# A two-block transformer layer on one core: pass loop folded into one, low weight parts multiplied first, the router's chain rearranged behind the last output fill, and each quad's first up half placed in front of its predecessor's spreading

## The reference

```python
h = h + merged @ w_out[l]
h = h + hier_moe(rms_norm(h, norm2_g[l]), w_router_group[l], b_router_group[l],
                 w_router_expert[l], b_router_expert[l], w_expert_in[l], w_expert_out[l])
return rms_norm(h, norm_f_g)

def hier_moe(...):                        # 4 groups of 8 experts, 2 experts per token
    g_sel = argmax(xt @ w_group + b_group)
    top_v, top_i = top_k(e_logits of the chosen group, 2)
    gates = g_prob * softmax(top_v)
    hdn = ragged_dot(xs, w_e_in, group_sizes)      # 32 experts, 1024 -> 2 x 256
    act = silu(gate_h) * up_h
    ys = ragged_dot(act, w_e_out, group_sizes)     # 256 -> 1024, times the gate, added to the token
```

## Time and profile before

| what | value |
|---|---|
| runs of the kernel | 960.22, 959.97, 955.93 us; median 959.97 |
| profiled execution | 960.35 us, of which the trace's span is 958.6 us |
| busy: PE, DVE, ACT, POOL | 858.6, 497.6, 391.0, 92.2 us |
| DMA | 217.57 MB, mean 227 GB/s |
| TensorE's granted clock, mean | 0.958 of full |

### The profile page before, as it was taken

How to read it: one execution, slowest core, us unless ns; L and a number is a source line. 1 busy time by engine, 2 the same in 40 slices (tenths; PEclk the granted TensorE clock), 3 DMA queues, 4 the chain that set the end, 5 groups by cost and what they waited for, 6 DMA issues and landing times.

```text
span 958.6 us, 14713 instructions
## 1 busy us (share of the span) xinstructions
PE 858.6 (90%) x5971; PEld 708.3 (74%) x5971; DVE 497.6 (52%) x779; ACT 391.0 (41%) x534; POOL 92.2 (10%) x111
## 2 busy tenths in 40 slices
PE   4889999899999986786668799999989899999996
PEld 3889789799997532332232698998888699999995
DVE  5798577654564311101010566455557557666674
ACT  5323453456342311101112455454643456566362
POOL 1032000111000000000001401111152000000000
PEclk9899999899999998987889799999999999999999
DMA  7755454224688999999999964424434816655611
GB/s 216 257 164 208 176 176 176 89 93 171 229 326 324 414 421 421 421 422 423 422 420 377 225 137 147 176 89 175 89 138 142 269 65 200 220 173 175 219 44 44
DMA packets 94392, 217.57 MB, mean 227 GB/s; under 512 B 14663, under 2 KB 45509, under 8 KB 82049
## 3 DMA queue, kind: packets, MB, share of 16 engines
q1 hardware_dynamic: 93649, 215.32, 61.9%
q10 hardware_dynamic: 576, 1.18, 0.4%
q0 software_dynamic: 112, 0.30, 0.3%
HBM read 215.44 MB, written 1.34 MB: 226 GB/s over the span
## 4 chain that ended last, share of the span: by engine, by line
PE 62%; DMA 16%; DVE 11%; ACT 4%; issue 4%; SPq 3%; POOL 0%; DVEq 0%; ACTq 0%
PE ps L826 14%; PE ps L828 14%; PE ps L827 14%; DMA moe_ring<-in_w_expert_in 14%; PE ps L1230 6%; PE ps L1147 5%; DVE w_lo L1607 3%; DMA stage<-in_w_in 1%; PE ps L985 1%; DMA stage_b<-in_w_up 1%; SPq L694 1%; ACT w_hi L1311 1%; PE ps L1179 1%; PE ps L1169 1%; PE ps L970 1%
## 5 line engine op out<-in xcount | busy, mean ns | idle before, releaser
L828 PE MATMUL ps<-x_hi,w_lo 128*128 128x256 f32 x664 | 189.8, 286 | 0.0
L828 PEld LDWEIGHTS ps<-x_hi,w_lo 128*128 128x128 f32 x664 | 129.5, 195 | 0.0
L1607 DVE TENSOR_TENSOR w_lo<-stage,w_hi 128x2048 fp32r<-128x2048 f32 (+1 forms) x44 | 101.8, 2354 | 32.1 <-ACT w_hi L1311 30.9
L826 PE MATMUL ps<-x_hi,w_hi 128*128 128x256 f32 x360 | 105.6, 293 | 8.8 <-DVE w_lo L1607 8.2
L1311 ACT ACTIVATE w_hi<-stage 128x2048 fp32r<-128x2048 f32 (+1 forms) x44 | 79.1, 1848 | 61.0 <-PE ps L828 51.7
L827 PE MATMUL ps<-x_lo,w_hi 128*128 128x256 f32 x360 | 103.9, 289 | 0.0
L826 PE MATMUL ps<-x_hi,w_odd 128*128 128x256 f32 x312 | 89.1, 285 | 1.3 <-DVE x_lo L1598 1.3
L828 PE MATMUL ps<-x_hi,w_odd 128*128 128x256 f32 x312 | 88.3, 283 | 0.0
L827 PE MATMUL ps<-x_lo,w_odd 128*128 128x256 f32 x312 | 88.3, 283 | 0.0
L826 PE MATMUL ps<-x_hi,w_lo 128*128 128x256 f32 x304 | 86.6, 285 | 0.0
L827 PE MATMUL ps<-x_lo,w_lo 128*128 128x256 f32 x304 | 86.0, 283 | 0.0
(11 more groups left out here) (381 smaller groups left out, 1915.6 us busy)
## 6 DMA issues: line engine op xcount, KB each, us to landing
stage<-in_w_in SPq DMA_DIRECT2D x23, 2048.0 KB, 8.1
moe_ring<-in_w_expert_in SPq DMA_DIRECT2D x44, 1024.0 KB, 18.1
moe_ring<-in_w_expert_out SPq DMA_DIRECT2D x20, 1024.0 KB, 19.4
stage_b<-in_w_up SPq DMA_DIRECT2D x12, 1024.0 KB, 8.6
stage<-in_w_down SPq DMA_DIRECT2D x11, 1024.0 KB, 5.0
stage<-in_w_up SPq DMA_DIRECT2D x10, 1024.0 KB, 9.5
up_odd<-in_w_expert_in SPq DMA_DIRECT2D x8, 1024.0 KB, 22.1
down_odd_a<-in_w_expert_out SPq DMA_DIRECT2D x6, 1024.0 KB, 21.0
```

Source lines behind the costliest of these rows:

```text
L826: mm(out, still[0], moving[0], start=first, stop=False)
L828: return mm(out, still[1], moving[0], start=False, stop=last)
L1607: tt(lo[:, cols], staged(n)[:, cols], hi[:, cols].bitcast(fp32), ALU.subtract).then_inc(lo_ready, 1)
```

## The change

1. SP's loads: `up_odd_c` lies at 160 KiB (before at 96), and is loaded with `up_odd_d` once `merged_ready` is 4; `wide_g` takes its place at 100 KiB, over tile 1 of h_tok, and is loaded by ACT behind the residuals. The second pair of quad 0's down pieces and one half of down_odd_b wait for a new semaphore `wo_read`.
2. The fourth wo fill multiplies in another order: the 8 products with w_lo first, then those with x_lo, then the high ones; after the first and the second eight, wo_read is raised. The same 9 products as before stand between the router's steps.
3. `route()`: PE takes the first half of the logits of tile 1 before the transposes; the rank's products are handed over one by one; three of the four residuals stand behind the first up half of quad 0. ACT takes tile 0's xs_tok before it squares tile 1; POOL adds EPS ahead.
4. The first up half of quad q+1 (`first_half`) stands in front of the spreading of quad q.
5. PE's passes are one loop whose count is 1 at first and is read from npass_i before the last two quads; an `If(r > 0)` holds the gather and first half that later passes need. The other engines keep the second copy.

```diff
-    steps.append({"op": "wopart", "k": range(0, 2)})
+    steps.append({"op": "wopart", "k": range(0, 6)})
     at("xt", 2)
-    steps.append({"op": "wopart", "k": range(2, 3)})
+    steps.append({"op": "wopart", "k": range(6, 9)})
...
             eng.wait_ge(merged_ready, 4)
-            load_up(1, 1, 0, range(3, 4))
+            load_up(1, 1, 0, high)
             wait_split(eng, units_one - 1)
             load_up(0, 0, 0, high)
             eng.wait_ge(pj_full, units[units_one - 2]["read"])
             load_up(0, 0, 1, low)
             load_down(0, 0, low)
+            eng.wait_ge(wo_read, 1)
+            load_down(0, 0, high)
+            eng.wait_ge(wo_read, 2)
+            load_down(1, 1, range(3, 4))
             eng.wait_ge(pj_full, units[units_one - 1]["read"])
             load_up(0, 0, 1, high)
-            load_down(0, 0, high)
-            load_down(1, 1, high)
-            eng.wait_ge(routed_xs, 2)
-            eng.wait_ge(residual_in, 4)
-            load_up(1, 1, 0, range(2, 3))
+            load_down(1, 1, range(2, 3))
             load_rest(0)
...
+            def wo_last(products):
                 n = where["wo", 3]
+                w = parts(split_pair(units_one - 1))
...
+                for at in products:
+                    k = at % KT
+                    b, f = ((0, 1), (1, 0), (0, 0))[at // KT]
+                    last = mm(ps[:, n % 4, :], (x_hi, x_lo)[b][:, k, P:2 * P], w[f][:, k, 0:BANK],
+                              start=(at == 0), stop=(at == 3 * KT - 1))
+                    if k == KT - 1 and at // KT < 2:
+                        last.then_inc(wo_read, 1)
...
                 eng.wait_ge(sel_ready, 1)
+                mm(ps[:, 1, 0:32], tri[:, 0:P], chosen[:, 0, :], start=True, stop=True).then_inc(rank_full, 1)
+                wait_read(eng, "at", "xt", 1)
+                router_logits(3, 1, range(0, 4))
                 eng.wait_ge(h_ready, 4)
-                mm(ps[:, 2, 0:32], tri[:, 0:P], chosen[:, 0, :], start=True, stop=True).then_inc(rank_full, 1)
...
+                for half in range(2):
+                    eng.wait_ge(xt_copied, half + 1)
+                    last = router_logits(3, 1, range(4 + 2 * half, 6 + 2 * half))
+                last.then_inc(lg_full, 1)
...
+            def first_half(it, p):
+                eng.wait_ge(act_ready, it + 1)
+                eng.wait_ge(xg_a, it + 1)
+                eng.wait_ge(moe_in[(0, 4)[p]], it * 32 + (64, 32)[p])
+                up_half(p, 0).then_inc(up_a, 1)
...
+                if not final:
+                    first_half(it + 1, 1 - p)
                 eng.wait_ge(spread_ready, it + 1)
...
-                def quads(r):
+                def quads(r, count):
                     with eng.Fori(0, QUADS // 2 - 1) as i:
                         for p in range(2):
                             quad(r, i * 2 + p, p)
+                    eng.wait_ge(npass_ready, 1)
+                    eng.reg_load(count, npass_i[0:1, 0:1])
                     quad(r, QUADS - 2, 0)
                     quad(r, QUADS - 1, 1, True)
-                quads(0)
-                eng.wait_ge(npass_ready, 1)
-                passes = eng.value_load(npass_i[0:1, 0:1], min_val=1, max_val=S // CAP)
-                with eng.If(passes > 1):
-                    with eng.Fori(1, passes) as r:
+                first_half(0, 0)
+                for b in range(1, 4):
+                    residual(b // 2, b % 2)
+                count = eng.alloc_register("passes")
+                eng.reg_mov(count, 1)
+                with eng.Fori(0, count) as r:
+                    with eng.If(r > 0):
                         gather(r * QUADS, r * QUADS + 1)
-                        quads(r)
+                        first_half(r * QUADS, 0)
+                    quads(r, count)
...
+                    if t == 0:
+                        eng.wait_ge(half_squares, NT)
+                        step(eng.tensor_scalar(half_ms, ss_half[:, 0:2 * NT:2], EPS, None, ALU.add))
                     eng.wait_ge(half_squares, 3 + t)
-                    step(eng.tensor_tensor(ms[:, one], ss_half[:, 2 * t:2 * t + 1], ss_half[:, 2 * t + 1:2 * t + 2], ALU.add))
-                    step(eng.tensor_scalar(ms[:, one], ms[:, one], EPS, None, ALU.add))
+                    step(eng.tensor_tensor(ms[:, one], ss_half[:, 2 * t + 1:2 * t + 2], half_ms[:, one], ALU.add))
```

More of the change, by code:

```diff
@@ L1063, in route @@
                 eng.wait_ge(sel_ready, 2)
-                mm(ps[:, 2, 32:64], tri[:, P:S], chosen[:, 0, :], start=True, stop=False)
-                mm(ps[:, 2, 32:64], tri[:, 0:P], chosen[:, 1, :], start=False, stop=True)
-                mm(ps[:, 2, 64:96], tri[:, P:S], chosen[:, 0, :], start=True, stop=False)
-                mm(ps[:, 2, 64:96], tri[:, P:S], chosen[:, 1, :], start=False, stop=True).then_inc(rank_full, 1)
-                residual(1, 0)
+                mm(ps[:, 2, 0:32], tri[:, 0:P], chosen[:, 1, :], start=False, stop=True).then_inc(rank_full, 1)
+                for t in range(NT):
+                    last = mm(ps[:, 3, 0:32], tri[:, P:S], chosen[:, t, :], start=(t == 0), stop=(t == 1))
+                last.then_inc(rank_full, 1)
+                residual(0, 0)
                 eng.wait_ge(pick_ready, 1)
@@ L1121, in gather, with up_half @@
                     last.then_inc((gather_a, gather_b)[half], 1)
+            def up_half(p, half, final=False):
+                for kk in range(4):
+                    k = 4 * half + kk
+                    for j in range(QUAD):
+                        last = mm(ps[CAP * j:CAP * (j + 1), 2, :], xg[p][:, k, CAP * j:CAP * (j + 1)],
+                                  expert_up(p, half, j, final)[:, kk, :], start=(k == 0), stop=(k == KT - 1),
+                                  skip_group_check=True)
+                return last
@@ new lines, in quad @@
+                if not final:
+                    gather(it + 1, it + 1)
+                eng.wait_ge(gate_pick_ready, it + 1)
+                eng.wait_ge(actf_ready, it + 1)
+                for t in range(NT):
+                    last = eng.transpose(ps[:, 3, t * P:(t + 1) * P],
+                                         pick_gate[:, t, :, :].rearrange("p e c -> p (e c)"), ident[:, :])
+                last.then_inc(spread_full, 1)
+                eng.wait_ge(xg_b, it + 1)
+                if final:
+                    eng.wait_ge(up_last_in, r * 64 + 64)
+                else:
+                    eng.wait_ge(moe_in[1], r * (64 * (QUADS - 1)) + q * 64 + 64)
@@ L1821, in route @@
                 eng.wait_ge(rank_full, 1)
-                step(stt(rank[:, 0, :], chosen[:, 0, :], far, ps[:, 2, 0:32], ALU.mult, ALU.add))
+                step(stt(rank[:, 0, :], chosen[:, 0, :], far, ps[:, 1, 0:32], ALU.mult, ALU.add))
                 pick_slots(0, 0).then_inc(first_picked, 1)
-                eng.wait_ge(xt_full, 1)
-                eng.tensor_copy(x_feat[1][:, 4:8, :], ps[:, 0, :].rearrange("p (k t) -> p k t", k=4)).then_inc(xt_copied, 1)
+                eng.wait_ge(xt_full, 2)
+                for half in range(2):
+                    eng.tensor_copy(x_feat[1][:, 4 + 2 * half:6 + 2 * half, :],
+                                    ps[:, 0, half * S:(half + 1) * S].rearrange("p (k t) -> p k t", k=2)).then_inc(xt_copied, 1)
                 first_rstd(1)
```

83 lines of the change are left out of this document (30 added, 53 removed).

## The result

The changed kernel takes 951.63 us (median of 6 runs, 950.1 to 953.39) against 959.22 (6 runs, 955.93 to 960.22): ratio 0.9929, 95% interval 0.9915 to 0.9944.

The account below looks back on a forecast made before the run. The prediction took DMA of expert weights to bound the expert stage, and TensorE's unexplained stop to follow it. Gains of 4.2 (loads, router), 4.3 (pass loop) and 1.0 (clock) made 9.5, from 960.35 to 951 us; range 947.8 to 956.3.

Parts of the forecast that it names:

- Loads and router: Weight stream into the expert stage: 4.8 us from closing holes in the loads, less 0.6 us lateness, net gain 4.2 us.
- Term (a): Weight loads at 285 to 295 us: issuing up_odd_c some 36 us earlier fills the holes, gain 2.5 us.
- this dryness: Weight queue near 320 us: the first up half ends at 320.4, 0.6 us later than the queue needs it.
- The choice: Router, VectorE choosing for the second token tile: starts at 310.8 instead of 312.05, 1.25 us earlier.
- the first up half: Quad 0, after routing: starts at 316.7 instead of 319.08 and ends at 320.4.
- First up half ahead of the spreading, and the If: Expert loop: the reorder is worth 0 us; the new branch before gather 1 costs 0, with 1.2 and 4.0 kept.
- The pass loop: Hand-over to the second block: without the second copy the stop goes, PE's first product at 535.7 instead of 540.05, 4.3 us.
- The clock: Second block's start, 536 to 544 us: less standing still restores part of the granted clock, 1.0 us (ends 0 and 2.1).
- The sum: Whole kernel: 4.2 + 4.3 + 1.0 = 9.5 us, taken from the profiled 960.35 to give 951.
- Rival 4: Slower: the new If's instruction fetch queues behind a full DMA queue, long stop before gather 1; 965 at 18 us; 5%.
- the forecast: Whole kernel: the outcome held likeliest, 949 to 953.5 us, with 62%.
- rival 2: Front gain eaten: the If costs 4.0 or quad 0 is late, stream hole at 333; 954.9 to 955.1 us; 13%.

Follow-up runs that it names:

- spread_first: The changed kernel, but each quad's first up half again behind its predecessor's spreading: 951.06 us, 0.9912 of the kernel before.
- loop_alone: The kernel before with only TensorE's new pass loop (count in a register, read ahead, If at the loop's start): 949.40 us, ratio 0.9911.
- two_copies: The changed kernel, but PE's further passes as a second copy, the count read at the end, as before: 954.06 us, 0.9947 of the kernel before.
- read_early: The kernel before with PE's count read ahead of the last two quads, the jump over the second copy kept: 956.91 us, ratio 0.9987.
- split_later: The changed kernel with ScalarE's split at the hand-over moved behind its squares and raw_hi: 946.80 us, 0.9891 of the kernel before.
- after_again: The changed kernel unaltered, measured once more on another run's chip: 950.92 us, 0.9924 of the kernel before.
- pad_96: The changed kernel with ScalarE's hand-over split moved later, plus 96 unawaited semaphore increments before TensorE's first wait: 944.83 us, 0.9855 of the kernel before.

## Why the prediction was right, and where its sum was not

- **Loads and router, 4.2.** Right in kind, a little large: 3.93 between the two profiles, 3.35 between the means of three kernels with the front and five without (+188.56 and +191.91). The inside was off. Term (a), 2.5 us for up_odd_c, was sized by the bytes that fit the hole of 285 to 295. It measured 0.5 to 0.9, and one reason is in the windows: the queue, emptied sooner, runs low at 320 to 330, since SyncE can issue the next pieces only at 318.91, behind the end of the first up half (318.68). The sum charged 0.6 for this dryness. So the other terms must hold the most of the gain; they were not undone singly. The choice came 1.34 us earlier (1.25 forecast), the first up half 2.41 in this profile (2.38) and 1.8 in three others.
- **First up half ahead of the spreading, and the If, 0.** Right: spread_first, and gather 1 without idle, behind the residuals in the kernel after and without their cover in loop_alone.
- **The pass loop, 4.3.** The mechanism was right: the jump makes the stop (two_copies 9.17, read_early 8.00 to the first product), a block of instructions loads inside it, and the new If, inside its own pass, pays nothing visible. The Trainium skill ("Runtime: NRT & Kernel Launch", Instruction fetch mechanics) says that a taken branch out of the loaded blocks has to wait for a fetch. The traces agree for this jump: the transposes start 2.8 to 2.9 us after the block. The size was off where the prediction let ScalarE's squares end at 533.84 "and then raw_hi": it kept these squares where they stood, while the front moved TensorE up by 4.2 us. Ahead of them in ScalarE's order stands a split that awaits a transfer, and that moved by less (1.9 us in the mean), in part because an instruction block ran among its weights. Measured 2.9 to 3.9 with the front, 3.9 to 4.9 without it. In split_later, where the wait is gone, it is 5.4.
- **The clock, 1.0.** Mis-sized: 0.4 in the first pair of profiles, -0.7 to 0.4 over the four kernels of this kind (16.29 to 17.42 against 16.69). It can give its 1.9, but repeats of one program differ in it.
- **The sum.** 3.35 + 3.4 (mean of 6.10, 5.25, 5.16 and 6.17 against 9.07) + 0 is 6.8 us, and the two measurements of the changed kernel gave 7.6 and 6.5. The forecast said 9.5, yet 951 held, since it was subtracted from a profiled run of 960.35, above every median of the kernel before (957.4 to 960.0). That is luck: from the median of 959.22 the same 9.5 give 949.7, and from 957.41 they give 947.9, where after_again measured 950.92.
- **What no term had:** the 2.8 us in the second layer. Nothing was lost there by the change; but an edit of TensorE's program length can win them, and loop_alone did. So most of the 4 to 6 us by which the two halves alone gain more than the whole is accounted for: 2.8 here, and 1.1 in front of the hand-over.
- **Small slips.** The sum lets the old gather start at 316.5, the row says 316.34. Rival 4 takes 9.3 for the whole gain, which is 9.5. By the prediction's own chances, the forecast and half of rival 2 are 0.685 and the rest within 0.5% is 0.265, not 0.75 and 0.20. None of this changes the forecast.

## What to carry to other kernels

When an edit brings a stage forward, list what each engine awaits at its end in program order: a wait that was covered by an old stop can become the bound, and an instruction that only prepares later work should not stand ahead of the ones the hand-over needs. Judge the parts of a change together as well as apart; here gains of 0.5% and 0.8 to 0.9% alone made 0.7 to 0.8% together. And before explaining 2 to 3 us in a place that an edit didn't touch, look for a row of instruction loading in the DMA table of that stretch, and for the granted clock.

## What the runs showed of the hardware

- A load of one block of TensorE's instructions (16 KB) among 2 MB of urgent weights delayed these by 1.0 to 1.4 us; behind the TensorE wait that this made longer (2.1 to 2.5 us instead of 1.1) the clock fell to the lower level (1.2 GHz) for a while, 2.8 us in all. In front of the hand-over such a block cost a transfer 1.1 us.
- A jump over a whole second copy of the expert pass stopped TensorE for 3.8 us, or 4.8 to 4.9 with the read of the count in front of it; the block loaded inside the stop. Leaving the pass loop at its end costs nothing visible: the transposes start at 524.75, the last spreading ends at 524.92.
- The position of such a load follows the length of the program ahead of it: 96 instructions more moved it out of the way, 64 nearly.
- An increment of a semaphore in TensorE's queue is not free: with 64, 96 and 222 the first matmul starts at 10.78, 15.66 and 35.08 us (7.63 without), so each takes 0.15 us, and the first 40 or so pass while TensorE waits anyway.
- Best of all versions is pad_96, 0.9855 of the kernel before. Its padding is fitted to this one program and shifts with every edit; split_later (0.9891) is the part to keep.
